# Loading x and the meta tokens already turned, with the sums of squares moved into the second chunk

## The chip, the cores and the metric

The kernel runs on one core of one Trainium2 chip. The metric is the device time of one execution in microseconds (us); before the change its median over three runs is 1341.67 us (1341.34 to 1343.68).

## The reference

One decoder layer over 256 real tokens of width D = 2048, with 16 learned meta tokens in front (and masked padding before them). In the cut below `h` is the 272 rows that count.

```
h = concat(pad, meta_tokens, x)                       # 16 + 256 rows that count
u = h * rsqrt(mean(h*h, -1) + EPS) * norm_attn_pre    # first RMSNorm
z = u @ w_in                                          # (2048, 8448): qa ka va qb kb vb ga gb
ya = differential attention(qa, ka, va, rel_bias)     # 8 heads, causal, two softmaxes
yb = sliding-window attention(qb, kb, vb, rel_bias, sinks)  # 16 query heads, 2 key heads
h = h + rmsnorm((sigmoid(ga)*(ya@w_branch_a) + sigmoid(gb)*(yb@w_branch_b)) @ w_out)
h = h + rmsnorm(square(relu(rmsnorm(h) @ w_ff1)) @ w_ff2)
return h[real tokens]
```

The part that matters here is the first norm and the first columns of `z`. The factor 1/rms of a row is one number per token, so the kernel leaves it out of `u` and multiplies it in after the product with `w_in`.

## The kernel before, in words

**Tiling.** Every large product is a sweep over chunks of a weight matrix. A chunk has eight units (`UNITS`), and a global count `tau = 8*c + u` numbers them: chunk 0 is units 0 to 7, chunk 1 units 8 to 15, and so on. Chunk 0 is the 256 columns of `w_in` for keys and values of the sliding-window attention (256 KB a unit). Chunk 1 is the first 512 query columns (512 KB a unit). A weight unit goes through four stations: SP issues its load into a slot of `raw` (eight slots), ScalarE (ACT) rounds it to `w_hi` (line 428), VectorE (DVE) subtracts to get the remainder `w_lo` (line 794), and TensorE (PE) multiplies high by high, low by high and high by low. In the same way the activations have a high part `u_hi` and a low part `u_lo`. PE raises the count `used` after each unit, and SP waits for `used` to reach `8c + u - 7` before it loads the unit that reuses that slot.

**Order.** Each engine has its own program written out in order. ACT and DVE run `LEAD = 5` units ahead: at step `tau` they prepare unit `tau + 5`, and extra jobs are placed at chosen steps, always ahead of that step's preparation. On PE the extra job of a step comes after that step's product.

**Chunk 0.** x lies in memory with tokens as rows, and the products want it turned. SP loads x as four pieces of 512 KB into `xs`. PE turns it: `turn_x` (four transposes of 128 x 128 a unit, line 1306), `turn_meta` (16 small ones, line 1395) and one transpose for the gain (line 1336), into banks of PSUM. ACT multiplies by the gain and rounds (`keep_x`, line 451), DVE keeps the remainder (`keep_x`, line 828). The two products of `bias_table` (line 1413) stand ahead of the first unit. Every second unit ACT and DVE each take the sum of squares of one piece of x (`square_x`, line 459, and line 843).

**The scales.** When the sums are there, DVE adds them (line 846), ACT takes the roots with a loaded table (lines 477 and 478), and DVE inverts and spreads them into `rstd_t` (lines 855 to 859), raising `scales_ready`. At the end of step `SCALES_AT` = 11 PE turns them (`turn_scales`, lines 1375 and 1376), and DVE keeps them as `rstd_bc` one step later (`keep_scales`, lines 866 and 868). The keys and values of chunk 0 are copied from banks 0 and 1 by `copy_first` at DVE's step 9 (line 878); PE waits for it before unit 12, the first that writes those banks again:

```
                        if u == 4:
                            pe.wait_ge(acc_free, 2 * c)
```

PE turns the keys and values at the end of step 14 (`TURN_AT`, lines 1425, 1381 and 1382). The first half of chunk 1's queries is taken out of PSUM at step 13: ACT copies one part (`copy_queries`, line 496), DVE adds and scales (`keep_queries`, lines 887 and 890) and raises `half_free`, for which PE waits before unit 16.

**GpSimd (POOL)** waits for chunk 0's last weights, issues six small loads (lines 383 to 385), stores the bias table (line 409) and then loads the bias of each attention job (line 397), the first two ahead and the rest job by job.

Of the kernel before, what the change touches and what calls it, by code (L numbers as in the profile page):

```python
# [89 lines left out]
UNTURNED = 8  # L90
# [27 lines left out]
def hybrid_block(nc, x, meta_tokens, rel_bias, w_in, w_branch_a, w_branch_b, w_out, lambda_q1, lambda_k1,  # L118
                 lambda_q2, lambda_k2, diff_norm, sinks, norm_attn_pre, norm_attn_post, w_ff1, w_ff2,
                 norm_ff_pre, norm_ff_post, identity, buckets, out):  # L120
# [3 lines left out]
    with ctx:  # L124
# [6 lines left out]
        def region(kb4, *groups):  # L131

            made = []
            for group in groups:
# [20 lines left out]
        (qaT, kbT, vb, vb_m, qbT, kaT, va, va_m), (_, va_lo2, vam_lo2), (_, sq_lo), (y_hi, y_lo), (f_hl,) = region(  # L155
# [6 lines left out]
            [("gap6", [P, 10274], F32), ("sq_lo", [P, SEQ], F32R)],  # L162
            [("y_hi", [P, KT, SEQ], F32R), ("y_lo", [P, KT, SEQ], F32R)],
# [4 lines left out]
        (yA, yT, t, pT, pTm, bias), (_, _, _, pTr, pTmr), (_, sq_hi), (m_hi, m_lo), (hid_hi, hid_lo), (xs,) = region(  # L168
# [8 lines left out]
            [("xs", [P, BLOCKS, D], F32)])  # L177


        (ga,), (_, vam_lo0, va_lo0, _, va_lo1), (og,), (facc,), (xm, g_rows, g_col, meta_g, relx, buck) = region(  # L180
# [4 lines left out]
            [("xm", [META, D], F32), ("g_rows", [KT, P], F32), ("g_col", [P, KT], F32),  # L185
             ("meta_g", [P, KT, META], F32), ("relx", [N_BUCKETS + 1, HA + HB], F32),
             ("buck", [N_BUCKETS + 1, 2, TAB], F32)])
# [18 lines left out]
        ident = sb("ident", [P, P])  # L206
        lam_v = sb("lam_v", [P, 4, DHA])
# [18 lines left out]
        x_landed = [sem(f"x_landed{i}") for i in range(4)]  # L226
# [8 lines left out]
        gain_turned, gain_ready = sem("gain_turned"), sem("gain_ready")  # L235
        meta_turned, meta_scaled = sem("meta_turned"), sem("meta_scaled")
        meta_hi_ready, meta_lo_ready = sem("meta_hi_ready"), sem("meta_lo_ready")
# [78 lines left out]
        def _(sp):  # L316
# [6 lines left out]
            sp.dma_start(ident[:], identity).then_inc(consts_landed, 16)  # L323
            sp.dma_start(g_rows[:], norm_attn_pre[0].rearrange("(k p) -> k p", p=P)).then_inc(consts_landed, 16)

            for u in range(UNITS):
                if u % 2 == 0:
                    cols = slice(u // 2 * CW, (u // 2 + 1) * CW)
                    sp.dma_start(xs[:, :, cols], xf[:, :, cols]).then_inc(x_landed[u // 2], 16)
                if u == 0:  # L330
                    sp.wait_ge(rel_ones, 1)
                    sp.dma_start(relx[0:N_BUCKETS, :], rel_bias).then_inc(rel_landed, 16)
                    sp.dma_start(buck[:], buckets).then_inc(rel_landed, 16)
                load(u, w_in, slice(u * 256, u * 256 + 256), slice(KB0, KB0 + 256), None, 256)
            for c in range(1, C_MIX):
                n0 = w_in_column(c)
                for u in range(UNITS):
                    if c < C_GA:
                        h, k0 = u // 4, (u % 4) * 4 * P
                        sp.wait_ge(used, 8 * c + u - 7)  # L340
                        sp.sem_inc(slot_free, 1)
                        sp.dma_start(fours(raw)[:, u], unit_of(w_in, slice(k0, k0 + 4 * P),
                                                              slice(n0 + h * 256, n0 + h * 256 + 256)))\
                          .then_inc(landed[u], 16)
                        continue
                    load(u, w_in, slice(u * 256, u * 256 + 256), slice(n0, n0 + CW), 8 * c + u - 7)
# [30 lines left out]
        def _(pool):  # L377
# [35 lines left out]
            pool.memset(pTmr[:].bitcast(F32), 0.0)  # L413
            pool.memset(vam_lo0[:].bitcast(F32), 0.0).then_inc(meta_zero, 1)
# [10 lines left out]
        def _(act):  # L425
# [16 lines left out]
            act.dma_start(xm[:], meta_tokens).then_inc(xm_landed, 16)  # L442
# [3 lines left out]
            def keep_x(i):  # L446

                act.wait_ge(turned, i + 1)
                for k in range(2):
                    kt = 2 * i + k  # L450
                    last = act.activation(u_hi[:, kt, 0:SEQ], bank[2 + i % 4][:, k * SEQ:(k + 1) * SEQ],
                                          ACT.Identity, scale=g_col[:, kt:kt + 1])
                last.then_inc(turned_hi, 1)

            def square_x(j):

                if j:
                    act.wait_ge(stats, j + 1)
                act.activation(gate_b[:, 0, :], xs[:, 0, j * CW:(j + 1) * CW], ACT.Square,
                               accum_out=ss3[:, j:j + 1]).then_inc(stats, 1)  # L460

            act.wait_ge(xm_landed, 16)
            act.activation(qaT[0:META].rearrange("p h t -> p (h t)"), xm[:], ACT.Square, accum_out=ssm[0:META, :]).then_inc(stats, 1)
            act.wait_ge(gain_ready, 1)
            act.wait_ge(meta_scaled, 1)
            act.activation(u_hi[:, :, SEQ:KEYS], meta_g[:], ACT.Copy).then_inc(meta_hi_ready, 1)
            for u in range(UNITS):
                keep_x(u)
                split_hi(u, 0, 256)
                if u % 2:  # L470
                    square_x(u // 2)

            for u in range(UNITS - LEAD, UNITS):
                split_ahead(0, u)
                if u == UNITS - LEAD + 2:
                    act.wait_ge(norm, 1)
                    act.activation(rstd, ssx, ACT.Sqrt, scale=1.0 / D, bias=eps).then_inc(stats, 1)
                    act.activation(rstdm[0:META, :], ssm[0:META, :], ACT.Sqrt, scale=1.0 / D, bias=eps[0:META, :])\
                       .then_inc(stats, 1)
# [303 lines left out]
        def _(dve):  # L783
# [28 lines left out]
            dve.wait_ge(gain_turned, 1)  # L812
            dve.tensor_copy(g_col[:], bank[7][:, 0:KT]).then_inc(gain_ready, 1)
            dve.wait_ge(gain_ready, 1)

            def scale_meta():

                dve.wait_ge(meta_turned, 1)
                gains = g_col[:].rearrange("p (k a) -> p k a", a=1).broadcast_to([P, KT, META])
                dve.tensor_tensor(meta_g[:], bank[6][:, 0:KT * META].rearrange("p (k t) -> p k t", k=KT), gains,  # L820
                                  ALU.mult).then_inc(meta_scaled, 1)

            def keep_x(i):

                dve.wait_ge(turned_hi, i + 1)
                for k in range(2):
                    kt = 2 * i + k
                    last = dve.scalar_tensor_tensor(u_lo[:, kt, 0:SEQ], bank[2 + i % 4][:, k * SEQ:(k + 1) * SEQ],
                                                    g_col[:, kt:kt + 1], u_hi[:, kt, 0:SEQ].bitcast(F32),
                                                    ALU.mult, ALU.subtract)  # L830
                last.then_inc(turned_lo, 1)

            scale_meta()
            dve.wait_ge(meta_hi_ready, 1)
            dve.tensor_tensor(u_lo[:, :, SEQ:KEYS], meta_g[:], u_hi[:, :, SEQ:KEYS].bitcast(F32), ALU.subtract)\
               .then_inc(meta_lo_ready, 1)

            for u in range(UNITS):
                keep_x(u)
                split_lo(u, u + 1, 256)  # L840
                if u % 2:
                    cols = slice(u // 2 * CW, (u // 2 + 1) * CW)
                    link(dve.tensor_tensor_reduce(rows[:, 1, :], xs[:, 1, cols], xs[:, 1, cols], 1.0, 0.0, ALU.mult,
                                                  ALU.add, ss3[:, 4 + u // 2:5 + u // 2]))
            dve.wait_ge(stats, 5)
            dve.tensor_reduce(ssx, ss3[:].rearrange("p (b j) -> p b j", b=BLOCKS), AX.X, ALU.add)\
               .then_inc(norm, 1)
            for u in range(UNITS - LEAD, UNITS - LEAD + 3):
                split_ahead(0, u)
            dve.wait_ge(table_ready, 1)  # L850
            for w in range(2):
                last = dve.tensor_copy(rows[0:HA + HB, w, 0:TAB], bank[6 + w][0:HA + HB, 0:TAB])
            last.then_inc(table_copied, 1)
            dve.wait_ge(stats, 7)
            link(dve.reciprocal(rstd, rstd))
            link(dve.reciprocal(rstdm[0:META, :], rstdm[0:META, :]))
            dve.tensor_scalar(rstd8, rstd, DHA ** -0.5, None, ALU.mult).then_inc(norm, 1)
            dve.tensor_copy(rstd_t[:, 0:2, :], rstd.rearrange("p (b a) -> p b a", a=1).broadcast_to([P, BLOCKS, P]))
            dve.tensor_copy(rstd_t[0:META, 2, :], rstdm[0:META, :].broadcast_to([META, P])).then_inc(scales_ready, 1)
            for u in range(UNITS - LEAD + 3, UNITS):  # L860
                split_ahead(0, u)
# [168 lines left out]
            def attention(tau):  # L1030
# [15 lines left out]
                if tau == 9:  # L1046
                    copy_first()
                if tau == SCALES_AT + 1:
# [253 lines left out]
        def _(pe):  # L1302
# [32 lines left out]
            pe.wait_ge(consts_landed, 32)  # L1335
            pe.transpose(bank[7][:, 0:KT], g_rows[:], ident[0:KT, 0:KT]).then_inc(gain_turned, 1)
# [34 lines left out]
            def turn_scales():  # L1371

                pe.wait_ge(scales_ready, 1)
# [18 lines left out]
            def turn_meta():  # L1392
                pe.wait_ge(xm_landed, 16)
# [348 lines left out]
```

## Time and profile before

| | |
|---|---|
| median of 3 runs | 1341.67 us |
| the profiled execution | 1341.08 us |
| its span, first to last instruction | 1339.3 us |
| TensorE busy | 1328.5 us (99%) |
| VectorE busy | 797.7 us (60%) |
| ScalarE busy | 628.1 us (47%) |
| GpSimd busy | 47.5 us (4%) |
| bytes moved | 252.60 MB, mean 189 GB/s |

Busy means that an instruction was in flight; it is not use at peak. 1.8 us of the time lie outside the span. Averages over the span say little about the change, which touches only about its first 50 us; the rows further down are of that stretch. In them an instruction has its start and its duration; in brackets stands the idle time of its engine just before it and what ended that. "x8" merges eight instructions. PEclk is the granted TensorE clock as a share of full.

### The profile page before, as it was taken

The page shows a single profiled execution, that of the slowest core. Times are in us where ns is not written, and L with a number is a line of the kernel's source. Part 1 is how long each engine was busy: PE and PEld are TensorE (multiplying, and loading weights), DVE is VectorE, ACT ScalarE, POOL GpSimd, SP SyncE. Part 2 cuts the span into 40 slices and gives each one's busy share as a digit, 9 for nine tenths or more (in the row PEclk, how much of TensorE's full clock was granted, in tenths as well). Part 3 has the DMA queues.
Part 4 walks back from the last instruction along what each step waited for, and adds up shares of the span by engine and source line. Part 5 has one row for each costly group of instructions (what it writes and reads, how often), then busy time and mean ns, then how long its engine had stood idle before and what let it go on. Part 6 is the DMA issues. An engine that isn't in the chain of part 4 may idle for free.

```text
span 1339.3 us, 19239 instructions
## 1 busy us (share of the span) xinstructions
PE 1328.5 (99%) x7157; PEld 1136.5 (85%) x7157; DVE 797.7 (60%) x1100; ACT 628.1 (47%) x909; POOL 47.5 (4%) x91
## 2 busy tenths in 40 slices
PE   9999999999999999999999999999999999999997
PEld 8889989888888888888988888888888888888886
DVE  7665564677775555557765545565546555456554
ACT  7454444455664434454644334443344444344442
POOL 1222110000000000000010000000000000000000
PEclk9999999999999999999999999999999999999999
DMA  9765555555566666774766666666666656666663
GB/s 295 203 183 166 166 161 155 160 167 150 159 191 188 188 195 206 232 239 150 251 188 194 195 190 189 189 191 195 193 189 189 189 190 194 195 190 188 191 192 107
DMA packets 146714, 252.60 MB, mean 189 GB/s; under 512 B 8483, under 2 KB 43727, under 8 KB 146236
## 3 DMA queue, kind: packets, MB, share of 16 engines
q1 hardware_dynamic: 142924, 241.39, 58.6%
q0 software_dynamic: 2160, 4.74, 1.8%
q10 hardware_dynamic: 1552, 5.37, 1.1%
q8 instruction: 56, 0.92, 0.3%
q14 instruction: 22, 0.18, 0.0%
HBM read 249.29 MB, written 2.17 MB: 188 GB/s over the span
## 4 chain that ended last, share of the span: by engine, by line
PE 98%; DVE 1%; DMA 0%; ACT 0%; issue 0%; SPq 0%; DVEq 0%; ACTq 0%
PE bank L1318 17%; PE bank L1320 17%; PE bank L1319 17%; PE bank L1648 16%; PE bank L1651 9%; PE bank L1366 4%; PE bank L1353 3%; PE bank L1354 3%; PE bank L1355 3%; PE bank L1368 2%; PE bank L1672 1%; PE bank L1306 1%; PE bank L1675 1%; PE bank L1457 1%; PE bank L1456 1%; DMA xs<-in_x 0%
## 5 line engine op out<-in xcount | busy, mean ns | idle before, releaser
L794 DVE TENSOR_TENSOR w_lo<-raw,w_hi 128x1024 fp32r<-128x1024 f32 (+1 forms) x456 | 549.8, 1214 | 432.8 <-ACT w_hi L428 430.9
L428 ACT ACTIVATE w_hi<-raw 128x1024 fp32r<-128x1024 f32 (+1 forms) x456 | 474.4, 1050 | 486.6 <-DMA raw<-in_w_ff 359.9
L1648 PE MATMUL bank<-f_hl,w_hi 128*128 128x512 f32 x960 | 229.8, 391 | 0.5 <-issue 0.5
L1648 PEld LDWEIGHTS bank<-f_hl,w_hi 128*128 128x128 f32 x960 | 176.3, 188 | 34.9 <-issue 0.9
L1318 PE MATMUL bank<-w_hi,hid_hi 128*128 128x512 f32 x512 | 199.2, 389 | 0.0
L1319 PE MATMUL bank<-w_lo,hid_hi 128*128 128x512 f32 x512 | 199.2, 389 | 0.0
L1320 PE MATMUL bank<-w_hi,hid_lo 128*128 128x512 f32 x512 | 199.2, 389 | 0.0
L1651 PEld LDWEIGHTS bank<-f_hl,w_lo 128*128 128x128 f32 x960 | 123.1, 191 | 4.7
L1651 PE MATMUL bank<-f_hl,w_lo 128*128 128x256 f32 x960 | 124.5, 283 | 0.0
L1320 PEld LDWEIGHTS bank<-w_hi,hid_lo 128*128 128x128 f32 x512 | 96.1, 188 | 20.0
L1319 PEld LDWEIGHTS bank<-w_lo,hid_hi 128*128 128x128 f32 x512 | 96.1, 188 | 20.0
L1318 PEld LDWEIGHTS bank<-w_hi,hid_hi 128*128 128x128 f32 x512 | 96.1, 188 | 19.9
L1318 PE MATMUL bank<-w_hi,u_hl 128*128 128x512 f32 x256 | 101.2, 395 | 0.0
L1320 PE MATMUL bank<-w_hi,u_hl 128*128 128x512 f32 x256 | 99.8, 390 | 0.0
L1319 PE MATMUL bank<-w_lo,u_hl 128*128 128x512 f32 x256 | 99.7, 390 | 0.0
L1353 PE MATMUL bank<-u_hl,w_hi 128*128 128x272 f32 x284 | 83.3, 293 | 0.2 <-DVE w_lo L794 0.2
L1354 PE MATMUL bank<-u_hl,w_lo 128*128 128x272 f32 x288 | 82.9, 288 | 0.0
L1355 PE MATMUL bank<-u_hl,w_hi 128*128 128x272 f32 x288 | 82.9, 288 | 0.0
L514 ACT ACTIVATE t<-t,sc 128x145 f32<-128x145 f32 (+1 forms) x64 | 29.3, 459 | 85.6 <-DVE sc L975 85.6
L1366 PE MATMUL bank<-u_hl,w_hi 128*128 128x512 f32 x256 | 62.8, 394 | 0.0
L1318 PEld LDWEIGHTS bank<-w_hi,u_hl 128*128 128x128 f32 x256 | 48.0, 188 | 12.2 <-issue 2.9
L1320 PEld LDWEIGHTS bank<-w_hi,u_hl 128*128 128x128 f32 x256 | 48.1, 188 | 10.3
(244 smaller groups left out, 1509.7 us busy)
## 6 DMA issues: line engine op xcount, KB each, us to landing
raw<-in_w_ff SPq DMA_DIRECT2D x256, 512.0 KB, 3.7
raw<-in_w_in SPq DMA_DIRECT2D x128, 512.0 KB, 3.7
raw<-in_w_out SPq DMA_DIRECT2D x32, 512.0 KB, 4.5
raw<-in_w_branch_b SPq DMA_DIRECT2D x16, 512.0 KB, 3.8
raw<-in_w_branch_a SPq DMA_DIRECT2D x16, 512.0 KB, 3.8
xs<-in_x SPq DMA_DIRECT2D x4, 512.0 KB, 6.5
raw<-in_w_in SPq DMA_DIRECT2D x8, 256.0 KB, 6.6
bias<-bias_table POOLq DMA_DIRECT2D x8, 256.0 KB, 4.6
```

The costliest lines, as they stand in the source:

```text
L428: act.activation(w_hi[:, u, :, 0:width], raw[:, u, :, 0:width], ACT.Copy).then_inc(hi_ready, 1)
L514: last = act.activation(t[:, e, a:b], t[:, e, a:b], ACT.Exp, bias=nmx[:, 2 * e + q:2 * e + q + 1], accum_out=sums[:, 2 * e + q:2 * e + q + 1])
L794: dve.tensor_tensor(w_lo[:, u, :, 0:width], raw[:, u, :, 0:width], w_hi[:, u, :, 0:width].bitcast(F32), ALU.subtract).then_inc(lo_ready, 1)
L1318: pe.matmul(ps[b][:, 0:width], hi_of(kt, b), wh, start=a, stop=False)
L1319: pe.matmul(ps[b][:, 0:width], hi_of(kt, b), wl, start=False, stop=False)
L1320: ins = pe.matmul(ps[b][:, 0:width], lo_of(kt, b), wh, start=False, stop=z)
L1353: pe.matmul(out, wh[:, k, cols], u_hi[:, kt, 0:KEYS], start=a, stop=False)
L1354: pe.matmul(out, wl[:, k, cols], u_hi[:, kt, 0:KEYS], start=False, stop=False)
L1355: ins = pe.matmul(out, wh[:, k, cols], u_lo[:, kt, 0:KEYS], start=False, stop=z)
L1366: ins = pe.matmul(out, wh[:, k, cols], u_hl[:, :, kt, 0:SEQ], start=kt == 0, stop=kt == KT - 1)
L1648: ins = pe.matmul(acc[g][:], w_hi[:, u, k, cols], f_hl[:, kt, :], start=kt == 0, stop=kt == KT - 1)
L1651: ins = pe.matmul(acc[g][:, 0:SEQ], w_lo[:, u, k, cols], f_hl[:, kt, 0:SEQ], start=False, stop=False)
```

## The change

`x` and the meta tokens come in turned, as a new input `turned_x` (2048 x 272) that is laid out on the host, and so does the gain, as `gain` (128 x 16). The core of the change:

1. The tile `xt` (128 x 16 x 272) takes the turned input, one piece of 272 KB a unit, each just ahead of that unit's weights on SP's queue. `keep_x` on ACT and DVE reads `xt` rather than PSUM, and covers 272 columns. All transposes of x, of the meta tokens and of the gain are gone, and so are `scale_meta` and what followed it.
2. The identity, the rows of x (`xs`, still 4 x 512 KB) and the meta tokens (`xm`) are loaded in the middle of chunk 1's weights on SP's queue. They now serve only the sums of squares and later transposes.
3. The sums of squares move to steps 9 to 12 on ACT and DVE, the meta tokens' to step 12 on ACT, the adding, the roots and the inversion to step 13.
4. `turn_scales` moves from step 11 to 14, the turn of keys and values from 14 to 16, the first taking of queries from 13 to 15.
5. The small table loads go to ACT's queue. The two products of the bias table come after units 0 and 1, and DVE copies the table out in unit 6 of chunk 0.
6. POOL waits for the scales (`norm` at 2) ahead of its last clearing, and so ahead of the first loads of bias.

```
-TURN_AT = {14: ("kvb", 0)}
-SCALES_AT = 11
+TURN_AT = {16: ("kvb", 0)}
+SCALES_AT = 14
+SQUARES_AT = {9: 0, 10: 1, 11: 2, 12: 3}
-QUERIES_AT = {8 * c + 5 + 4 * h: (c, h) for c in QUERIES for h in range(2)}
+QUERIES_AT = {8 * c + (5 if c > 1 or h else 7) + 4 * h: (c, h) for c in QUERIES for h in range(2)}
...
# SP
-            sp.dma_start(ident[:], identity).then_inc(consts_landed, 16)
-            sp.dma_start(g_rows[:], norm_attn_pre[0].rearrange("(k p) -> k p", p=P)).then_inc(consts_landed, 16)
             for u in range(UNITS):
-                if u % 2 == 0:
-                    cols = slice(u // 2 * CW, (u // 2 + 1) * CW)
-                    sp.dma_start(xs[:, :, cols], xf[:, :, cols]).then_inc(x_landed[u // 2], 16)
...
+                sp.dma_start(xt[:, UK * u:UK * u + UK, :], turned_x[u * UK * P:(u + 1) * UK * P].rearrange("(k p) t -> p k t", p=P))\
+                  .then_inc(x_landed[u], 16)
                 load(u, w_in, slice(u * 256, u * 256 + 256), slice(KB0, KB0 + 256), None, 256)
...
+                        if c == 1 and u >= 3 and u < 7:
+                            cols = slice((u - 3) * CW, (u - 2) * CW)
+                            sp.dma_start(xs[:, :, cols], xf[:, :, cols]).then_inc(rows_landed[u - 3], 16)
+                        if c == 1 and u == 3:
+                            sp.dma_start(ident[:], identity).then_inc(consts_landed, 16)
+                        if c == 1 and u == 6:
+                            sp.dma_start(xm[:], meta_tokens).then_inc(xm_landed, 16)
...
# POOL, ahead of the last memset and the first loads of bias
+            pool.wait_ge(norm, 2)
...
# ACT
+            act.dma_start(g_col[:], gain).then_inc(gain_landed, 16)
+            act.wait_ge(rel_ones, 1)
+            act.dma_start(relx[0:N_BUCKETS, :], rel_bias).then_inc(rel_landed, 16)
+            act.dma_start(buck[:], buckets).then_inc(rel_landed, 16)
...
-                act.wait_ge(turned, i + 1)
...
+                act.wait_ge(x_landed[i], 16)
+                for kt in (2 * i, 2 * i + 1):
+                    last = act.activation(u_hi[:, kt, 0:KEYS], xt[:, kt, :], ACT.Identity, scale=g_col[:, kt:kt + 1])
...
+                    if 8 * c + u in SQUARES_AT:
+                        square_x(SQUARES_AT[8 * c + u])
+                    if 8 * c + u == 12:
+                        square_meta()
+                    if 8 * c + u == 13:
+                        root_x()
...
# DVE
             for u in range(UNITS):
                 keep_x(u)
                 split_lo(u, u + 1, 256)
...
+                if u == 6:
+                    dve.wait_ge(table_ready, 2)
+                    for w in range(2):
+                        last = dve.tensor_copy(rows[0:HA + HB, w, 0:TAB], bank[6 + w][0:HA + HB, 0:TAB])
+                    last.then_inc(table_copied, 1)
...
+                if tau in SQUARES_AT:
+                    square_rows(SQUARES_AT[tau])
+                if tau == 13:
+                    sum_rows()
+                    keep_roots()
...
# PE
-            turn_meta()
-            turn_x(0)
-            turn_x(1)
-            bias_table()
-            pe.wait_ge(meta_hi_ready, 1)
...
                 multiply_turned(u, w_hi[:, u], w_lo[:, u], [u * UK + k for k in range(UK)], acc_of(0), high=u > 0)
-                if u == 0:
-                    turn_x(2)
-                if u + 3 < UNITS:
-                    turn_x(u + 3)
+                if u < 2:
+                    bias_table(u)
```

## Rows read from the trace of the kernel before

**Rows 1.** The page's busy times, and of its groups DVE's costliest (busy, mean ns | idle).
```profile
PE 1328.5 (99%) x7157; PEld 1136.5 (85%) x7157; DVE 797.7 (60%) x1100; ACT 628.1 (47%) x909; POOL 47.5 (4%) x91
...
L794 DVE TENSOR_TENSOR w_lo<-raw,w_hi 128x1024 fp32r<-128x1024 f32 (+1 forms) x456 | 549.8, 1214 | 432.8 <-ACT w_hi L428 430.9
```

**Rows 2.** Who waited for whom on PE, whole span: us in total, times, longest.
```profile
PE bank L1331 <- DVE rows L809: 1.2, 1, 1.2
```

**Rows 3.** Timeline, PE, chunk 0 and start of chunk 1.
```profile
7.49 1.52 PE L1413 MATMUL bank<-buck,relx 33*24 33x400 f32 x4
8.94 0.77 PE L1342 MATMUL bank<-u_hl,w_hi 128*128 128x272 f32 x4
10.80 1.03 PE L1306 MATMUL bank<-ident,xs 128*128 128x128 f32 x8
24.44 2.11 PE L1366 MATMUL bank<-u_hl,w_hi 128*128 128x512 f32 x8
```

**Rows 4.** Timeline, POOL, chunk 0 to the bias table's store.
```profile
17.32 0.67 POOL L383 DMA_DIRECT2D lam_v<-in_lambda_q  x1 [16.29 <-DMA raw<-in_w_in]
28.26 0.61 POOL L409 DMA_DIRECT2D bias_table<-rows  x1 [7.62 <-DMA sink_bc<-in_sinks]
```

**Rows 5.** Timeline, DVE, chunks 0 and 1.
```profile
13.77 0.87 DVE L828 SCALAR_TENSOR_TENSOR u_hl<-bank,g_col,u_hl 128x256 fp32r<-128x256 f32 x2
26.57 1.04 DVE L852 COPY rows<-bank 24x400 f32<-24x400 f32 x2
27.53 0.14 DVE L855 RECIPROCAL sc<-sc 128x2 f32<-128x2 f32 x1
28.18 0.21 DVE L859 COPY gate_b<-sc 16x128 f32<-16x128 f32 x1
31.72 0.77 DVE L878 COPY gate_b<-bank 128x272 f32<-128x272 f32 x2
36.28 0.44 DVE L866 COPY rstd_bc<-bank 128x272 f32<-128x272 f32 x1
38.53 0.75 DVE L887 TENSOR_TENSOR rows<-bank,rows 128x256 f32<-128x256 f32 x2
```

**Rows 6.** Timeline, ACT, chunks 0 and 1.
```profile
4.34 1.91 ACT L463 ACTIVATE qaT<-xm 16x2048 f32<-16x2048 f32 x1 [1.64 <-DMA xm<-in_meta_tokens]
21.34 0.63 ACT L459 ACTIVATE gate_b<-xs 128x512 f32<-128x512 f32 x1
21.96 2.95 ACT L428 ACTIVATE w_hi<-raw 128x1024 fp32r<-128x1024 f32 x3
24.93 1.28 ACT L477 ACT_TABLE_LOAD   x1
26.42 0.28 ACT L478 ACTIVATE sc<-sc 16x1 f32<-16x1 f32 x1
29.06 1.06 ACT L428 ACTIVATE w_hi<-raw 128x1024 fp32r<-128x1024 f32 x1 [0.33 <-DMA raw<-in_w_in]
32.22 1.06 ACT L428 ACTIVATE w_hi<-raw 128x1024 fp32r<-128x1024 f32 x1 [0.20 <-DMA raw<-in_w_in]
```

**Rows 7.** Windows: busy us of each engine, then PEclk, DMA share, GB/s.
```profile
10.00:15.00 5.00, 4.77 (x40) 4.56 (x39) 4.18 (x10) 4.07 (x12) 0.00 (x0) 1.00 1.06 380
20.00:25.00 5.00, 5.00 (x39) 4.84 (x38) 4.86 (x10) 4.89 (x9) 0.64 (x2) 1.00 0.91 178
```

**Rows 8.** Timeline, PE, end of step 11 to step 15.
```profile
35.70 0.38 PE L1375 MATMUL bank<-ident,gate_b 128*128 128x128 f32 x2
36.17 2.11 PE L1366 MATMUL bank<-u_hl,w_hi 128*128 128x512 f32 x8
44.73 1.14 PE L1425 MATMUL bank<-gate_b,ident 128*64 128x272 f32 x8
46.10 1.19 PE L1368 MATMUL bank<-u_hl,w_lo 128*128 128x256 f32 x8
```

**Rows 9.** Window near the span's end, columns as in Rows 7.
```profile
1334.00:1336.00 2.00, 0.00 (x0) 0.00 (x0) 2.00 (x4) 0.00 (x0) 0.00 (x0) 0.86 0.40 154
```

More of the change, by code:

```diff
@@ L89 @@
 T_Y = 8
-UNTURNED = 8
+UNTURNED = 16
 T_M = T_Y + 8
@@ L119, in hybrid_block @@
                  lambda_q2, lambda_k2, diff_norm, sinks, norm_attn_pre, norm_attn_post, w_ff1, w_ff2,
-                 norm_ff_pre, norm_ff_post, identity, buckets, out):
+                 norm_ff_pre, norm_ff_post, identity, buckets, turned_x, gain, out):
     table = nc.dram_tensor("bias_table", (2, HA + HB, TAB), F32)
@@ L206, in hybrid_block @@
         ident = sb("ident", [P, P])
+        g_col = sb("g_col", [P, KT])
+        junk = xt[:].rearrange("p k t -> p (k t)")[:, 0:2 * CW].rearrange("p (b n) -> p b n", b=BLOCKS)
         lam_v = sb("lam_v", [P, 4, DHA])
@@ L223, in hybrid_block @@
         S0, S1, TB, MB = bank[4:8]
-        x_landed = [sem(f"x_landed{i}") for i in range(4)]
+        x_landed = [sem(f"x_landed{u}") for u in range(UNITS)]
+        rows_landed = [sem(f"rows_landed{i}") for i in range(4)]
         xm_landed, consts_landed, zeros_set = sem("xm_landed"), sem("consts_landed"), sem("zeros_set")
@@ L457, in square_x, with square_meta @@
                 if j:
-                    act.wait_ge(stats, j + 1)
-                act.activation(gate_b[:, 0, :], xs[:, 0, j * CW:(j + 1) * CW], ACT.Square,
+                    act.wait_ge(stats, j)
+                act.wait_ge(rows_landed[j], 16)
+                act.wait_ge(turned_lo, UNITS)
+                act.activation(junk[:, 0, :], xs[:, 0, j * CW:(j + 1) * CW], ACT.Square,
                                accum_out=ss3[:, j:j + 1]).then_inc(stats, 1)
[L462 to L466, printed above, removed]
+            def square_meta():
+                act.wait_ge(xm_landed, 16)
+                act.activation(kaT[0:META].rearrange("p h t -> p (h t)")[:, 0:D], xm[:], ACT.Square,
+                               accum_out=ssm[0:META, :]).then_inc(stats, 1)
+            act.wait_ge(gain_landed, 16)
             for u in range(UNITS):
@@ L469, in _, with root_x @@
                 split_hi(u, 0, 256)
-                if u % 2:
-                    square_x(u // 2)
             for u in range(UNITS - LEAD, UNITS):
                 split_ahead(0, u)
[L475 to L479, printed above, removed]
+            def root_x():
+                act.wait_ge(norm, 1)
+                act.activation(rstd, ssx, ACT.Sqrt, scale=1.0 / D, bias=eps).then_inc(stats, 1)
+                act.activation(rstdm[0:META, :], ssm[0:META, :], ACT.Sqrt, scale=1.0 / D, bias=eps[0:META, :])\
+                   .then_inc(stats, 1)
             def root_lam():
@@ L810, in _, with square_rows @@
             dve.memset(eps, EPS).then_inc(eps_set, 1)
[L812 to L821, printed above, removed]
             def keep_x(i):
                 dve.wait_ge(turned_hi, i + 1)
[L826 to L830, printed above, removed]
-                last.then_inc(turned_lo, 1)
[L833 to L836, printed above, removed]
+                for kt in (2 * i, 2 * i + 1):
+                    last = dve.scalar_tensor_tensor(u_lo[:, kt, 0:KEYS], xt[:, kt, :], g_col[:, kt:kt + 1],
+                                                    u_hi[:, kt, 0:KEYS].bitcast(F32), ALU.mult, ALU.subtract)
+                last.then_inc(turned_lo, 1)
+            def square_rows(j):
+                dve.wait_ge(rows_landed[j], 16)
+                cols = slice(j * CW, (j + 1) * CW)
+                link(dve.tensor_tensor_reduce(junk[:, 1, :], xs[:, 1, cols], xs[:, 1, cols], 1.0, 0.0, ALU.mult,
+                                              ALU.add, ss3[:, 4 + j:5 + j]))
+            dve.wait_ge(gain_landed, 16)
             for u in range(UNITS):
@@ L840, in _ @@
                 split_lo(u, u + 1, 256)
[L841 to L847, printed above, removed]
@@ L848, in _ @@
-            for u in range(UNITS - LEAD, UNITS - LEAD + 3):
-                split_ahead(0, u)
[L850 to L861, printed above, removed]
+                if u == 6:
[3 more added lines that the diff above has]
+                    last.then_inc(table_copied, 1)
@@ new lines, in _, with sum_rows, keep_roots @@
+            for u in range(UNITS - LEAD, UNITS):
+                split_ahead(0, u)
+            def sum_rows():
+                dve.wait_ge(stats, 5)
+                dve.tensor_reduce(ssx, ss3[:].rearrange("p (b j) -> p b j", b=BLOCKS), AX.X, ALU.add)\
+                   .then_inc(norm, 1)
+            def keep_roots():
+                dve.wait_ge(stats, 7)
+                link(dve.reciprocal(rstd, rstd))
+                link(dve.reciprocal(rstdm[0:META, :], rstdm[0:META, :]))
+                dve.tensor_scalar(rstd8, rstd, DHA ** -0.5, None, ALU.mult).then_inc(norm, 1)
+                dve.tensor_copy(rstd_t[:, 0:2, :], rstd.rearrange("p (b a) -> p b a", a=1).broadcast_to([P, BLOCKS, P]))
+                dve.tensor_copy(rstd_t[0:META, 2, :], rstdm[0:META, :].broadcast_to([META, P])).then_inc(scales_ready, 1)
@@ L1390, in turn_values, with bias_table @@
                 ins.then_inc(va_turned, 1)
[L1392 to L1415 removed]
+            def bias_table(w):
+                pe.wait_ge(rel_landed, 32)
+                pe.matmul(bank[6 + w][0:HA + HB, 0:TAB], relx[:], buck[:, w, :], start=True,
+                          stop=True).then_inc(table_ready, 1)
             def turn_rows(kind, i):
@@ L1733 @@
     given["buckets"] = bucket_table()
+    given["turned_x"] = np.ascontiguousarray(np.concatenate([given["x"][0].T, given["meta_tokens"].T], axis=1))
+    given["gain"] = np.ascontiguousarray(given["norm_attn_pre"][0].reshape(KT, P).T)
     arrays, args = {}, []
```

48 lines of the change are left out of this document (9 added, 39 removed).

## The prediction

> **What bounds the kernel now.** First the page's busy times [rows 1]: PE is busy 99% of the span, DVE 60%, ACT 47%. Then the waits of PE [rows 2]: over the whole span the largest is the 1.2 us before its first instruction. So PE sets the time from the first product on, and there are only two ways to change it: take work off PE, or make PE wait. The timeline of PE [rows 3] shows what may go: the first product is at 8.94 us, chunk 1 begins at 24.44, and transposes lie between the products. The timelines of ACT and DVE with the windows [rows 5 to 7] then show how close the other stations run here. At 10 to 15 us DMA is full (share 1.06, 380 GB/s), and in chunk 1 ACT still waits for weights (0.33 us before unit 13, 0.20 before unit 15). The bound of this stretch is PE, but with a full DMA queue just behind it. That is where I look for the answer.
>
> **Part 1, the head.** Removed from PE: eight groups of x's transposes at about 0.5 us (4 between 10.80 and the next product cost half of 1.03), the meta tokens' and the gain's. The 1.45 us of the bias table [rows 3] only move behind units 0 and 1. The end of chunk 0 then follows from what it waits for. Before, chunk 0's last weights were there at 17.3 us [rows 4]. The bytes in front of them hardly change: x turned with meta is 2.23 MB, in place of x (2.10), meta (0.13) and identity (0.07). After them DVE has the table's copy (26.57 to 27.53, 1.0) [rows 5], `keep_x` (0.9) and a half-size remainder (0.6, half of the mean 1.2 [rows 1]), then PE its last unit, 12 products at 0.125 us (1.5). With some overlap: 17.3 + 3.5 = 20.8 us. **Chunk 0 ends at 20.8 rather than 24.4: 3.6 us saved.** The saving is kept if nothing later waits.
>
> **Part 2, the queue of loads.** Each piece of x's rows is 524 KB, 1.4 us at 380 GB/s [rows 7]. Before, they were in chunk 0; now they lie in between units 11 to 15, and the turned x has taken their place. Bytes that must land before unit 13: before 4.50 (chunk 0) + 6 x 0.52 = 7.6 MB; now 4.44 + 3.15 + two row pieces and the identity 1.11 = 8.7 MB. That is 1.1 MB or 2.8 us more, so 29.06 becomes about 31.9 us [rows 6]. For unit 15: 8.7 MB before, and 4.44 + 4.19 + 2.10 + 0.20 = 10.9 MB now, 2.2 MB or 5.9 us more: 32.22 becomes 38.1. This presumes that the queue is full throughout, before and after. At 20 to 25 us only 178 GB/s moved, yet the share of busy DMA engines was 0.91 [rows 7], while POOL's six small loads were under way (they ended at 28.2, [rows 4]): I take this as engines held by slow packets, a loss that comes again, not as room.
>
> The Trainium skill ("DMA: Bandwidth & Descriptors", section "Issuing engines are not separate DMA queues") says that loads started from different engines run on the same 16 DMA engines and only save time at issue. It speaks against this change: loading x twice costs its bytes wherever they are issued. The 0.91 share at 178 GB/s agrees with it.
>
> **Part 3, the new waits.** Three things wait for those weights.
>
> First, `copy_first` is at DVE's step 9, behind the remainder of unit 13. Before it came at 31.72 [rows 5], 4 us ahead of PE's end of unit 11 (35.70, [rows 8]). Now: unit 13 lands 31.9, ACT 1.06, DVE 1.2, the copy 0.8: 34.9. A unit of chunk 1 takes 2.82 us on PE ((35.70 - 24.44)/4, [rows 3, 8]), so PE ends unit 11 at 20.8 + 11.3 = 32.1 and waits 2.8 us before unit 12.
>
> Second, the scales. `turn_scales` is in PE's queue behind unit 14, and all of PE's later work behind it. What it waits for stands on ACT behind the preparation of unit 17. From unit 15's landing, on ACT in order: preparation of 15 (1.0), a square (0.65), preparation of 16 (1.0), a square (0.65), the meta square (1.95, from 1.91 and its readout), preparation of 17 (1.05); the prices are from [rows 6] (2.95 for three preparations; 21.34 to 21.96 for a square). Sum 6.3, to 44.4. Units 16 and 17 land 1.4 and 2.8 us behind unit 15 and do not add. Then DVE's remainder of unit 17 (1.2) and the sum (0.2): 45.8. The table load and roots (24.93 to 26.70, 1.8, [rows 6]): 47.6. The inversions and spreading (27.53 to 28.39, 0.9, [rows 5]): **the scales are ready at 48.4.** PE ends unit 14 at 34.9 + 8.5 = 43.4 and waits 5.0 us. Before, the squares lay behind PE's own transposes and the roots were out by 28.4, 7 us ahead of PE. Taking 14 rather than 11 gives three units, 8.5 us, and the chain has grown later by 20.
>
> Third, `half_free`, ahead of unit 16. DVE after 48.4: remainders of 18 and 19 (2.4, the first waiting 0.2 for ACT), the scales' copy and first product (1.1, of the 2.25 between 36.28 and 38.53 without the remainder in between), the two additions (0.75): 53.0. PE turns the scales (0.47, [rows 8]), does unit 15 and is at 51.7: it waits 1.3 us.
>
> **The sum.** Unit 16 ends at 53.0 + 2.8 = 55.8, the turn of keys and values (44.73 to 46.10, 1.4, [rows 8]) leads to unit 17 at 57.2. Before, unit 17 began at 46.10 + 2 x 2.82 = 51.7. The difference, 3.6 gained less waits of 2.8 + 5.0 + 1.3, is +5.5 us. From unit 17 on the same products follow, and the other jobs keep their steps.
>
> I add 0.3 for the clock: at 1334 to 1336 us, where PE ran nothing, the granted clock averaged 0.86 [rows 9] against 1.00 in chunk 1 [rows 7], so it fell from 2.4 to 1.2 GHz there. Unit 15 at half clock would take up to 2.8 us more, of which 1.3 lie in the wait that follows: bounds 0 and +1.5. I take the low side, as PE's idle time here is the shorter one.
>
> The Trainium skill ("TensorE: Matmul & The Clock Gate", section "Why this matters for your kernels") likewise says that an idle PE falls back to half its clock. The trace agrees for the span's end; no row of before shows it between products.
>
> Parts priced at nothing: DVE's squares (0.7 each, inside its waits for ACT and the weights); POOL's later loads of bias, issued from about 49 us and landing within some 8 us of that, where the first job's maximum is at step 21, past 65 us; ACT's three more loads at the start, which lie before its first input lands. Cover gone, each costs its own few tenths, the bias loads nothing until 10 us late.
>
> So 1341.08 + 5.8 = **1346.9 us** for an execution like the profiled one, whose 1341.08 lies 0.6 below the median of 1341.67; I keep 1346.9.
>
> **The rivals.**
>
> *The low rate was room (B).* If 20 to 25 us was lack of requests, not slow packets, the now full queue makes up 5 - 0.9/0.38 = 2.7 us. Scales at 45.7, wait before unit 12 gone, `half_free` at 50.3, unit 17 at 54.5: +2.8, so 1343.9. For it: loads were held back by `used` there. Against: the share of 0.91.
>
> *The head's gain stays (C), faster.* The place is the wait for `scales_ready` behind unit 14. PE would be there at 20.8 + 7 x 2.82 = 40.5, so unit 15 must land by about 30 us, 8 before my sum; then nothing waits, and the price is -3.7: 1337.4. It decides from there on: every us later than 40.5 of the scales takes one off the gain, and from 44 on the change loses. For it: 60% of DVE and 47% of ACT say that there is room on average, and PE never waited before. Against: the bytes alone, 10.9 MB at 380 GB/s, take 28.7 us from a start at 3 to 4.
>
> *Later still (D).* The same waits with row pieces that land 3 us later, since they run beside POOL's small loads, or unit 15 wholly at half clock: +8.5, 1349.6.
>
> **How the numbers follow.** Chances: forecast 0.60, B 0.14, C 0.14, D 0.08, between B and C (chain and gain cancel) 0.04. A measurement of this kernel tells about 0.2%, 2.7 us, from no change. Faster: C, 0.14 and a little of the in-between, 0.15. Slower: forecast, D and over half of B, 0.76. Same: the rest, 0.09. The range takes in B and D and leaves C out: 1341.5 to 1350.
>
> **What would show it.** Right: chunk 1 starts on PE near 21; PE is idle near 32 to 35 before unit 12, and for about 5 us ending near 48.4 before `turn_scales`, released by DVE's spreading of the scales; ACT's meta square lies near 42; the waits list names DVE for some 9 us. Wrong: no idle time on PE after 21, or ACT getting unit 15 by 32 despite the row pieces ahead; then C or B holds. If chunk 1 starts later than 22, part 1 is mis-sized, though the end would not move, as the loads set it.

## The result, and the profile after

Over 20 runs each, the changed kernel takes 1345.53 us (1344.36 to 1346.73) and the kernel before 1342.91 us (1341.17 to 1346.97). The ratio is 1.0018, with a 95% interval of 1.0012 to 1.0025: the change makes the kernel slower by 0.1 to 0.25%, about 2.4 us. The two profiled executions lie further apart: spans of 1343.2 and 1339.3 us, 3.9 us. Part of the reason is the scatter of the kernel before. Of its 20 runs, 8 lie above 1345 us and 12 below 1344 (median 1342.27), while those of the changed kernel fill one band; the medians are 2.6 us apart, and 3.3 us when only the lower band is counted. The rest is that the profiled execution of before, 1341.08 us, is quicker than all 20 runs, and that of the changed kernel, 1344.97, is 0.6 below its median. Where sizes are compared below they are differences of spans, of one execution each; the ratios have all runs in them. How far single executions can be trusted shows in the start of chunk 1: PE's work in chunk 0 is the same in the eleven profiled executions of this document that load x turned, and chunk 1 starts in them between 20.16 and 21.14 us.

The page after, its busy times and its chain by engine:

```profile
PE 1326.1 (99%) x7108; PEld 1133.3 (84%) x7108; DVE 796.7 (59%) x1097; ACT 628.1 (47%) x908; POOL 48.0 (4%) x91
...
PE 96%; DMA 1%; DVE 1%; SPq 1%; ACT 1%; issue 0%; DVEq 0%; ACTq 0%
```

PE is 2.4 us less busy than in [rows 1], as work was taken from it, and still the span is longer. The chain that ended last now runs through DMA, SP's queue, ACT and DVE for about 4% of the span (PE's share is 96%, before it was 98%). PE's waits name the places (us in total, times, longest):

```profile
PE bank L1382 <- DVE gate_b L864: 4.9, 1, 4.9
PE bank L1339 <- DVE rows L821: 1.2, 1, 1.2
PE bank L1372 <- DVE gate_b L881: 0.9, 1, 0.9
```

In [rows 2] only the second of these was there. The timeline of PE after, to be read against [rows 3, 8]:

```profile
20.76 2.01 PE L1372 MATMUL bank<-u_hl,w_hi 128*128 128x512 f32 x8
...
30.09 2.00 PE L1372 MATMUL bank<-u_hl,w_hi 128*128 128x512 f32 x8
32.96 2.14 PE L1372 MATMUL bank<-u_hl,w_hi 128*128 128x512 f32 x8 [0.87 <-DVE gate_b L881]
...
40.49 1.11 PE L1374 MATMUL bank<-u_hl,w_lo 128*128 128x256 f32 x8
46.53 0.51 PE L1382 MATMUL bank<-ident,gate_b 128*128 128x128 f32 x2 [4.93 <-DVE gate_b L864]
...
47.19 2.08 PE L1374 MATMUL bank<-u_hl,w_lo 128*128 128x256 f32 x8
49.06 4.31 PE L1372 MATMUL bank<-u_hl,w_hi 128*128 128x512 f32 x16
...
54.25 1.14 PE L1413 MATMUL bank<-gate_b,ident 128*64 128x272 f32 x8
...
55.62 1.19 PE L1374 MATMUL bank<-u_hl,w_lo 128*128 128x256 f32 x8
```

Chunk 1 starts 3.7 us sooner (20.76, before 24.44). Unit 12 waits for `copy_first` (32.96), `turn_scales` waits 4.93 us for the scales (46.53). Eight products of 256 columns then take 2.08 us where they took 1.1, so PE runs at half clock (the granted clock is 0.50 from 47 to 50 us). Unit 17 begins at 55.62, 3.9 us later than before (46.10 and two units of 2.82, [rows 8]): the whole difference of the spans is made by then.

The chain behind the 4.93 us, on ACT and then DVE, and SP's issues of row pieces with the long landing behind them (from the chain that ended last):

```profile
29.89 1.06 ACT L430 ACTIVATE w_hi<-raw 128x1024 fp32r<-128x1024 f32 x1 [1.62 <-DMA raw<-in_w_in]
...
37.08 1.06 ACT L430 ACTIVATE w_hi<-raw 128x1024 fp32r<-128x1024 f32 x1 [1.99 <-DMA raw<-in_w_in]
...
40.22 1.90 ACT L470 ACTIVATE kaT<-xm 16x2048 f32<-16x2048 f32 x1
...
42.12 1.04 ACT L430 ACTIVATE w_hi<-raw 128x1024 fp32r<-128x1024 f32 x1
43.17 1.28 ACT L483 ACT_TABLE_LOAD   x1
```

```profile
32.12 0.78 DVE L881 COPY gate_b<-bank 128x272 f32<-128x272 f32 x2
...
43.26 1.23 DVE L806 TENSOR_TENSOR w_lo<-raw,w_hi 128x1024 fp32r<-128x1024 f32 x1 [1.30 <-ACT w_hi L430]
44.40 0.15 DVE L854 TENSOR_REDUCE sc<-ss 128x2 f32<-128x8 f32 x1
45.10 0.17 DVE L860 RECIPROCAL sc<-sc 128x2 f32<-128x2 f32 x1 [0.55 <-ACT sc L484]
...
45.76 0.62 DVE L864 COPY gate_b<-sc 16x128 f32<-16x128 f32 x1
```

```profile
18.88 2.80 SPq L341 DMA_DIRECT2D xs<-in_x  x1
...
23.61 2.52 SPq L341 DMA_DIRECT2D xs<-in_x  x1
```

```profile
26.93 10.13 DMA raw<-in_w_in
```

Unit 15's weights were issued only at 26.93, though `used` was at 8 by 20.9: SP was held in its own queue by the row pieces, whose issue took 2.80 and 2.52 us for the third and fourth, after 0.51 and 1.10 for the first two; unit 14's weights between them took 1.78 (21.79). Unit 15's weights landed at 37.08. From there the three preparations, two squares, the meta square, the remainder, the roots and the spreading follow one another to 46.4. The windows, with columns as in [rows 7]:

```profile
20.00:25.00 5.00, 5.00 (x35) 4.56 (x34) 3.29 (x3) 1.87 (x2) 0.00 (x0) 1.00 0.91 195
25.00:30.00 5.00, 5.00 (x31) 4.44 (x30) 1.23 (x1) 1.18 (x2) 0.61 (x1) 1.00 1.04 383
...
40.00:45.00 5.00, 1.60 (x11) 1.28 (x9) 3.21 (x7) 4.85 (x9) 0.00 (x0) 1.00 1.02 353
45.00:50.00 5.00, 3.47 (x14) 3.00 (x15) 4.80 (x11) 4.38 (x7) 4.29 (x10) 0.67 0.39 88
```

DMA is full from 25 to 45 us; ACT and DVE work 1.2 of 5 us at 25 to 30, waiting for weights, and ACT 4.85 of 5 at 40 to 45, when PE stands still from 41.6 on. The granted clock is at 2.4 GHz until 45 and averages 0.67 of it in the last row, after PE had run nothing from 41.6 to 46.5.

### The profile page after: what moved, and what is told of

It reads as the page before. It is cut to its first block, busy times and chain, and to the rows that moved or that the text cites. A ratio compares the mean times of both kernels' runs of the same rounds, so it can differ in the third digit from the quotient of the medians.

```text
span 1343.2 us, 19145 instructions
## 1 busy us (share of the span) xinstructions
PE 1326.1 (99%) x7108; PEld 1133.3 (84%) x7108; DVE 796.7 (59%) x1097; ACT 628.1 (47%) x908; POOL 48.0 (4%) x91
## 4 chain that ended last, share of the span: by engine, by line
PE 96%; DMA 1%; DVE 1%; SPq 1%; ACT 1%; issue 0%; DVEq 0%; ACTq 0%
PE bank L1326 17%; PE bank L1328 17%; PE bank L1327 17%; PE bank L1628 16%; PE bank L1631 9%; PE bank L1372 3%; PE bank L1359 3%; PE bank L1361 3%; PE bank L1360 3%; PE bank L1374 2%; PE bank L1652 1%; DMA raw<-in_w_in 1%; PE bank L1655 1%; PE bank L1445 1%; PE bank L1444 1%; SPq L341 1%
## 5 line engine op out<-in xcount | busy, mean ns | idle before, releaser
L1326 PEld LDWEIGHTS bank<-w_hi,u_hl 128*128 128x128 f32 x256 | 48.0, 188 | 12.2 <-issue 2.9
L1359 PEld LDWEIGHTS bank<-u_hl,w_hi 128*128 128x128 f32 x284 | 53.4, 188 | 4.0 <-issue 2.0
## 6 DMA issues: line engine op xcount, KB each, us to landing
xs<-in_x SPq DMA_DIRECT2D x4, 512.0 KB, 11.6
```

The costliest lines, as they stand in the source:

```text
L1326: pe.matmul(ps[b][:, 0:width], hi_of(kt, b), wh, start=a, stop=False)
L1359: pe.matmul(out, wh[:, k, cols], u_hi[:, kt, 0:KEYS], start=a, stop=False)
```

## The experiments

**Theory:** the head's gain is real, and the row pieces in the queue of weights together with the chain of squares and roots make PE wait for more than that. **Rivals:** the squares alone do it; the clock does it; the low rate at 20 to 25 us is lack of requests, not POOL's small loads. Each kernel was timed beside the kernel before on the same chip.

### Neither row loads nor their squares

```
-                            sp.dma_start(xs[:, :, cols], xf[:, :, cols]).then_inc(rows_landed[u - 3], 16)
...
-                act.activation(junk[:, 0, :], xs[:, 0, j * CW:(j + 1) * CW], ACT.Square, ...)
+                act.activation(junk[:, 0, 0:1], <one column of xt>, ACT.Square, ...)
```

DVE's squares are cut to one column in the same way.

> The changed kernel without the four loads of x's rows, and with the sums of squares of the real rows cut to one column (so the scales are wrong numbers; meta square, roots and all waits stay). My theory: the head's gain of 3.6 us is real and only later waits ate it, so PE waits neither before unit 12 nor before turn_scales, and the time is 3.5 to 3.7 us below the kernel before. Rival (the head was never worth anything, the time is set elsewhere): within 1 us of the kernel before.

Measured: 1337.89 us, ratio 0.9962 (0.9948 to 0.9975); span 1335.9, 3.4 below the kernel before. Of PE's waits in chunk 1 one of more than 0.2 us is left:

```profile
PE bank L1377 <- DVE gate_b L859: 0.3, 1, 0.3
```

The head's gain is real, and what undoes it is the rows, loaded and squared: 7.3 us of span between this kernel and the changed one.

### The row loads without the squares, and the squares without the loads

The first keeps `xs` and its four loads and squares one column of it; the second squares 512 columns of `xt` and has no loads.

> The changed kernel with the row loads as they are, but the sums of squares of the real rows cut to one column (the scales are wrong numbers). My theory, the queue of loads is the larger part: the wait before unit 12 stays (0.9 us), scales ready near 44.6 instead of 46.4, PE waits about 3 us for them, total 0.5 to 1.5 us above the kernel before. Rival, the squares on ACT and DVE are the cause: no wait for the scales, 3 us or more below the kernel before.

> The changed kernel with squares of full size late, but of data already on the chip, and no loads of x's rows (the scales are wrong numbers). My theory: units 13 to 15 land 4 to 6 us sooner, scales ready near 41, PE waits at most 0.5 us, about 3.3 us below the kernel before. Rival, ACT's chain is the cause: scales still after 44, no gain over the kernel before.

Measured, loads only: 1344.97 us, ratio 1.0016 (1.0005 to 1.0026), span 1342.7. Squares only: 1338.55 us, ratio 0.9967 (0.9956 to 0.9978), span 1337.3. PE's turn of the scales in the first and in the second:

```profile
45.41 0.66 PE L1382 MATMUL bank<-ident,gate_b 128*128 128x128 f32 x2 [4.14 <-DVE gate_b L864]
```

```profile
41.65 0.41 PE L1377 MATMUL bank<-ident,gate_b 128*128 128x128 f32 x2 [0.87 <-DVE gate_b L859]
```

Against the kernel with neither, by the spans, the squares cost 1.4 us, the loads 6.8, both 7.3. Counted from the start of chunk 1 to that of unit 17, which leaves out the scatter of the head, it is 1.0, 6.8 and 6.8. So the squares are hidden as long as the weights come late, which rules out the first rival. My expectations missed on both sides. For loads only, 0.5 to 1.5 us above the kernel before became 2.1 by the ratio and 3.4 by the spans: the scales came at 45.3, not 44.6, and PE, idle for 4.1 us, ran on at half clock. For squares only, a wait of at most 0.5 us became 0.87.

### The meta square early

```
-                        if c == 1 and u == 6:
+                        if c == 1 and u == 1:
                             sp.dma_start(xm[:], meta_tokens).then_inc(xm_landed, 16)
...
             for u in range(UNITS - LEAD, UNITS):
                 split_ahead(0, u)
+                if u == UNITS - 2:
+                    square_meta()
```

> The changed kernel with the meta tokens loaded behind unit 9 and squared on ACT behind the preparation of unit 11, where ACT waits for weights. My theory: the chain behind unit 15's landing is 2.1 us shorter, scales near 44.6, PE idle for about 3 us so that the granted clock stays at full, then a short wait for half_free: 2.5 to 3 us below the changed kernel. Rival (ACT's order does not matter since the weights' landing sets it): no difference from the changed kernel.

Measured: 1342.38 us, ratio 0.9994 (0.9984 to 1.0004), span 1341.0, 2.2 below the changed kernel. The size is near what I expected (0.6 us of it is that chunk 1 started at 20.16), but the way is another: I had PE idle for 3 us at the scales and its clock at full. The wait moved to unit 12, and with it the half clock (window 30 to 35 us, clock 0.85):

```profile
34.88 3.78 PE L1371 MATMUL bank<-u_hl,w_hi 128*128 128x512 f32 x8 [3.38 <-DVE gate_b L880]
```

```profile
30.00:35.00 5.00, 1.62 (x8) 1.03 (x6) 3.33 (x5) 2.19 (x5) 1.41 (x2) 0.85 1.07 393
```

PE then came to `turn_scales` after the scales and did not wait. The load or the square had made unit 13 late (31.81, after 29.89). Which of them, the last experiment tells.

### POOL's small loads later

```
-            pool.wait_ge(landed[UNITS - 1], 16)
-            <the six small loads>
...
             pool.wait_ge(norm, 2)
+            <the six small loads>
             pool.memset(vam_lo0[:].bitcast(F32), 0.0).then_inc(meta_zero, 1)
```

> The changed kernel with POOL's six small loads moved behind the scales instead of behind chunk 0's last weights. If they hold the DMA engines, as I took it in the prediction: units 12 to 17 land about 3 us sooner, no wait before unit 12, scales near 43.3, 2.5 to 3.5 us below the changed kernel and about 0.8 below the kernel before. Rival (the low rate at 20 to 25 us was lack of requests): unit 12 still lands after 26.5 us and the time is the changed kernel's.

Measured: 1341.11 us, ratio 0.9983 (0.9974 to 0.9992), span 1339.7, 3.5 below the changed kernel. The window of the low rate, and ACT's preparation of unit 12 (27.20 in the changed kernel):

```profile
20.00:25.00 5.00, 5.00 (x35) 4.62 (x34) 3.40 (x3) 2.19 (x3) 1.41 (x2) 1.00 1.07 391
```

```profile
24.80 1.06 ACT L430 ACTIVATE w_hi<-raw 128x1024 fp32r<-128x1024 f32 x1 [2.47 <-DMA raw<-in_w_in]
```

391 GB/s in place of 195: in the changed kernel the small loads had held the engines, so the third rival falls there. They cost unit 12 2.4 us, and unit 15 3.2 (33.84, after 37.08). Against the changed kernel that is the upper end of what I expected; against the kernel before I had 0.8 us below, and it is 2.3 below by the ratio and 0.4 above by the spans. The scales came at 42.7, and PE still waited 2.34 us for them and ran on at half clock. The Trainium skill ("DMA: Bandwidth & Descriptors", section "Rules for kernel authors") says that small transfers are mostly overhead and should be joined; the trace agrees that they cost far more than their bytes, with 2.4 us for some 140 KB in six loads (0.4 us at 391 GB/s); what joining them would give, no run here shows. The kernel before with the same move:

> The kernel before, with POOL's six small loads moved behind the clearing of its buffers. My theory: weights land up to 3.7 us sooner from unit 12 on but PE did not wait for any, so within 0.3 us of the kernel before. Rival (they cost time there too): 1 us or more below it.

Measured: 1342.13 us, ratio 0.9998 (0.9985 to 1.0011). There PE waits for no weights, and the same cost was hidden. Its window tells what the low rate of 178 GB/s before was made of:

```profile
20.00:25.00 5.00, 5.00 (x43) 4.92 (x41) 4.84 (x11) 4.42 (x9) 0.00 (x0) 1.00 0.89 288
```

288 GB/s without the small loads, not 391. About half of what was missing was the small loads; the other half fits the weights that waited for `used`, so for the kernel before the third rival holds in part.

### PE kept busy while it waits

```
                 pe.wait_ge(consts_landed, 16)
+                for _ in range(19):
+                    pe.matmul(MB[:, 0:P], ident[:], ident[:], start=True, stop=True)
                 pe.wait_ge(scales_ready, 1)
```

> The changed kernel with 19 products of 128 x 128 (identity by identity, f32, to a free bank) ahead of PE's wait for the scales, so that PE is not idle there. If the fall of the granted clock at 46 to 50 us costs 1.4 us: clock 1.00 throughout, unit 15 takes 2.8 us, 1.0 to 1.4 us below the changed kernel. Rival (half_free would make PE wait anyway): no difference.

Measured: 1344.12 us, ratio 1.0008 (1.0000 to 1.0017), span 1342.3, 0.9 below the changed kernel.

```profile
41.87 4.40 PE L1381 MATMUL bank<-ident 128*128 128x128 f32 x38
46.68 0.44 PE L1384 MATMUL bank<-ident,gate_b 128*128 128x128 f32 x2 [0.41 <-DVE gate_b L864]
...
47.21 1.22 PE L1374 MATMUL bank<-u_hl,w_lo 128*128 128x256 f32 x8
```

The 19 products show as 38 instructions. The scales are as late, the clock stays at 2.4 GHz, and from 47.2 to the turn of keys and values PE needs 6.26 us (47.21 to 53.47) instead of 7.06 (47.19 to 54.25). So half clock costs 0.8 us, less than the 1.0 to 1.4 that I had expected: part of it lies where PE would have waited for `half_free`. As the rest of the loss stays, the clock is not the cause but a surcharge.

### Both repairs, and a better order

> The changed kernel with the meta square early and POOL's small loads late. My theory: scales near 41.2, PE waits about 0.7 us for them and 0.5 for half_free: 2.5 to 3.5 us below the kernel before, so faster than both. Rival (the small loads now collide with the bias loads or with weights that PE needs): PE waits between units 16 and 24, and no gain over the kernel before.

Measured: 1339.48 us, ratio 0.9972 (0.9960 to 0.9983), span 1338.1; PE waits 1.23 us for the scales and 0.62 before unit 16. The changes made to it next:

```
-SQUARES_AT = {9: 0, 10: 1, 11: 2, 12: 3}
+SQUARES_AT = {9: (0,), 10: (1,), 11: (2, 3)}
...
-                if tau == 13:
+                if tau == 12:
                     sum_rows()
                     keep_roots()
-                if tau == SCALES_AT + 1:
+                if tau == SCALES_AT - 1:
                     keep_scales()
```

with the roots at ACT's step 12, the first queries at step 13, the meta load behind unit 11, the identity behind unit 12, and the meta square behind the preparation of unit 12.

> From the kernel with meta square early and small loads late: the meta load behind unit 11 and its square behind the preparation of unit 12, the last two squares at step 11, sum and roots at step 12, the scales and the first queries kept at DVE's step 13. My theory: scales ready near 40.3, PE at the end of unit 14 near 40.8, so neither the 1.2 us wait for the scales nor the 0.6 us for half_free is left: 1.0 to 1.8 us below the kernel it starts from. Rival (the two squares before unit 16's preparation, or DVE waiting for PE's turn at step 13, make weights late): PE waits for w_lo after unit 15 and nothing is gained.

> The same kernel as x7_both, for a comparison on one chip: near 1339.5 us.

Measured on one chip: 1337.01 us (1336.72 to 1337.40), ratio 0.9952 (0.9936 to 0.9968), beside 1339.62 us, ratio 0.9971 (0.9961 to 0.9981). It is faster than both kernels of the change: 5.8 us below the median before, 4.0 in spans. All waits of PE of more than 0.2 us, and the turn of the scales:

```profile
PE bank L1340 <- DVE rows L821: 1.2, 1, 1.2
PE bank L1315 <- DVE f_hl L816: 0.5, 1, 0.5
PE bank L1629 <- issue: 0.3, 1, 0.3
```

```profile
40.16 0.41 PE L1383 MATMUL bank<-ident,gate_b 128*128 128x128 f32 x2
```

Nothing is left between chunk 0 and the end but waits that the kernel before had too. The gain over the start kernel was 2.6 us rather than the 1.0 to 1.8 expected. From the start of chunk 1 to that of unit 17 it is 1.5 us (28.9 to 27.4), as expected; the rest is for the most part that chunk 1 began 0.7 us sooner (20.40, not 21.14), for which no run shows the cause.

### The meta load early, its square where it was

This parts the load from the square in the wait before unit 12.

> The changed kernel with only the load of the meta tokens (16 partitions, 128 KB) moved behind unit 9; its square stays at step 12. If such a load holds a few DMA engines for long: unit 11 lands about 2 us later than in the changed kernel, unit 13 near 31.8 instead of 29.9, and PE's wait before unit 12 grows to 2.5 to 3.5 us, with unit 15 nearly where it was. Rival (the square between the preparations made unit 12 late): unit 13 at most 0.4 us later, by its bytes.

Measured: 1344.15 us, ratio 1.0009 (1.0000 to 1.0019), span 1342.3. ACT's preparation of unit 11, at 22.08 in the changed kernel, and PE's unit 12:

```profile
24.74 1.06 ACT L430 ACTIVATE w_hi<-raw 128x1024 fp32r<-128x1024 f32 x1 [3.23 <-DMA raw<-in_w_in]
```

```profile
34.66 2.98 PE L1372 MATMUL bank<-u_hl,w_hi 128*128 128x512 f32 x8 [2.93 <-DVE gate_b L881]
```

So it was the load: 128 KB over 16 partitions delay unit 11 by 2.7 us (24.74 less 22.08), where by their bytes at 385 GB/s they would take 0.3. It does not need the small loads beside it: with those late, unit 11 is prepared from 21.26 when the meta load is late and from 23.38 and 23.18 when it is early, about 2.0 us. That it holds a few engines fits this but is not shown, as no view here names single engines.

## Why the prediction came out as it did

The direction, the place and the mechanism of the loss were right: idle PE before unit 12 and at `turn_scales`, released by DVE's copy and by DVE's spreading of the scales, because the row pieces stand ahead of the weights. The size was too large, +5.8 us against +3.9 in the spans and +2.4 by the ratio. Term by term, in the profiled execution:

| step | predicted | measured |
|---|---|---|
| start of chunk 1, against before | -3.6 | -3.7 |
| unit 13 prepared by ACT from | 31.9 | 29.9 |
| wait before unit 12 | 2.8 | 0.9 |
| unit 15 prepared by ACT from | 38.1 | 37.1 |
| from there to the scales | 10.3 | 9.3 |
| wait for the scales | 5.0 | 4.9 |
| wait for `half_free` before unit 16 | 1.3 | none shown |
| units 15 and 16 beyond 5.64 us | 0.3 | 1.4 |
| unit 17 later by | 5.8 | 3.9 |

**Part 1 came out by luck.** Chunk 1 started at 20.76, predicted 20.8, but not for the reason given. I had let chunk 0's last weights set its end (17.3 + 3.5). They were there by 16.0, DVE had the last remainder of chunk 0 by 18.6, and PE took up that unit at 19.3. PE had waited last here:

```profile
9.19 0.36 PE L1359 MATMUL bank<-u_hl,w_hi 128*128 128x272 f32 x1 [0.50 <-DVE w_lo L806]
```

From there to 20.76 PE ran without a wait, so its own products and the bias table set the end. What is gained is the work taken off PE; that the sum by the weights gives the same time is chance.

**Part 2 was mis-sized.** I had assumed that the queue was as full before as after, so that added bytes are added time: 2.8 us for unit 13, 5.9 for unit 15. They came 0.8 and 4.9 later. Before, units 12 and 13 had been held back by `used` (unit 13 was issued at 21.66, after the change at 18.35), so that part of what I counted as time of bytes was lack of requests. My rival B had half of it. The kernel before moved 178 GB/s at 20 to 25 us and 288 without its small loads, the changed kernel 195 and 391, so the low rate before was both lack of requests and small loads, and after the change it was the small loads. The part of the small loads came again after the change, as I had taken it.

**The chain to the scales was 1.0 us shorter.** I had put the table load behind DVE's sum, as it stands behind the wait in the program. It ran at 43.17, while DVE was still at unit 17's remainder (43.26 to 44.4): ACT loads its table ahead of the wait. From the sum to the first inversion there are 0.7 us (44.40 to 45.10) rather than 1.8. Where the meta square is early and the small loads late, the table is in place at 39.73 and ACT then waits for DVE's sum:

```profile
40.47 0.30 ACT L484 ACTIVATE sc<-sc 128x2 f32<-128x2 f32 x1 [0.74 <-DVE sc L853]
```

**The third wait changed into half clock.** With PE at half clock until about 50 us, `half_free` came in time. With the clock held up (19 extra products) a gap of 0.26 us is back before unit 16, not 1.3: DVE needed 3.8 us from the scales to `half_free` (46.4 to 50.2), where I had 4.6. My 0.3 for the clock and 1.3 for the wait were 1.6 together; measured are 1.4, all of them in the two units themselves.

The end hangs on the scales. They were ready at 46.4 rather than 48.4, 1.0 us from unit 15's landing and 1.0 from the chain, and from there to unit 17 it took 9.2 us where I had 9.1. These are the 1.9 us between +5.8 and +3.9, and the range had room for them. The error at unit 12 did not reach the end, as PE then waits for the same scales.

The other 1.5 us, from +3.9 to the +2.4 of the ratio, are no matter of the mechanism: they are the upper band of the kernel before, of which none was among the three runs that I had, and a profiled execution of it that was quicker than all of its 20 runs. The chance of 0.76 for slower by over 0.2% was too high for a change that measured 0.18%.

What stays open: where that upper band of the kernel before comes from. It is there too when only its small loads are moved (3 of 12 runs above 1346), but not clearly in any kernel that loads x turned (the widest of them spans 3.0 us, the best one 0.7). Runs of the upper band, in the timings beside the experiments, have spans of 1343.7 to 1345.1 us at a granted clock of 0.998 or 0.999, like the others: the time is lost inside the span and not by the clock. I have no profile of such a run.

## What to carry to other kernels

Work moved off a saturated engine pays only until the next queue: before moving loads into a stretch in which DMA is full, list what stands behind them in the issuing queue, and what waits for that in the engines' own orders; here 2 MB of loads and an in-order chain of 9 us took back 7.3 us from a gain of 3.4. A result that PE needs at a fixed step is best not placed behind the preparation of units that are needed only later. Small or narrow loads belong where nobody waits: the same six loads cost 3.5 us in one order and nothing in the other.

## What was not expected of the hardware

- Loading 128 KB over 16 partitions amid a full queue delayed the weights behind it by 2.7 us (unit 11 from 22.08 to 24.74), about eight times what its bytes would take.
- The issue itself can take long: the four row pieces of 512 KB held SP for 0.51, 1.10, 2.80 and 2.52 us, and delayed the issue of the weights behind them. With POOL's small loads later the last two took 1.69 and 1.68. A busy DMA alone does not do it: the 19 weight issues of the kernel before between 11 and 58 us, in part at 380 GB/s, took 0.37 each. There every load waits for a slot first, and lands 5.8 us after its issue in the median, the row pieces 11.6; that the number of loads under way decides is not shown.
- The activation table for the roots is loaded ahead of the wait of the instruction that needs it, so its 1.28 us are hidden if ACT arrives early (loaded from 43.17, the awaited sum began at 44.40).
- PE's clock was at half after idle stretches of 4.9, 4.1, 3.4, 2.9 and in one kernel 2.3 us, and stayed at full after those of 1.8, 1.3, 1.2 and 0.9 us.
